# Expert weights eight rows to a partition, with the gathered tokens turned at a step of eight columns

## The reference

```python
def expert_choice_moe(h, w_router, w_gate, w_up, w_down):
    cap = EC_FACTOR * n // N_EXPERTS
    aff = jax.nn.softmax(jnp.einsum('bnd,de->bne', h, w_router), axis=-1)
    g, idx = lax.top_k(jnp.swapaxes(aff, 1, 2), cap)
    xs = jax.vmap(lambda hb, ib: hb[ib])(h, idx)
    hid = jax.nn.silu(jnp.einsum('becd,edf->becf', xs, w_gate)) * jnp.einsum('becd,edf->becf', xs, w_up)
    y = jnp.einsum('becf,efd->becd', hid, w_down) * g[..., None]
    return jax.vmap(lambda yb, ib: jnp.zeros((n, d)).at[ib.reshape(-1)].add(yb.reshape(-1, d)))(y, idx)
```

## Time and profile before

| | |
|---|---|
| median of 3 runs | 6196.72 us (6195.44 to 6198.15) |
| the profiled execution | 6197.2 us |
| its span, first to last instruction | 6195.5 us, so 1.7 us lie around it |
| mean granted clock of TensorE | 0.893 of full speed |
| TensorE busy | 5059.5 us, 82% of the span |
| VectorE, ScalarE, GpSimd busy | 31%, 18%, 17% |
| bytes by DMA | 491.31 MB, of which 32 x 3 loads of 2 MB are expert weights |

### The profile page before, as it was taken

How to read it: one execution, slowest core, us unless ns; L and a number is a source line. 1 busy time by engine, 2 the same in 40 slices (tenths; PEclk the granted TensorE clock), 3 DMA queues, 4 the chain that set the end, 5 groups by cost and what they waited for, 6 DMA issues and landing times. The chain is left out here.

```text
span 6195.5 us, 88364 instructions
## 1 busy us (share of the span) xinstructions
PE 5059.5 (82%) x37782; PEld 3656.2 (59%) x37782; DVE 1949.5 (31%) x2498; ACT 1102.5 (18%) x1784; POOL 1054.0 (17%) x782
## 2 busy tenths in 40 slices
PE   7689885888978879999695698799996956984897
PEld 2578764788833557777362276637664422763675
DVE  0206455444442142233303543241112035425001
ACT  1314212222221020000301132210001112312111
POOL 0120113434410212323000201101112002010011
PEclk8899997899998989999796799799997977996998
DMA  6220101000044111111000000276661100002985
GB/s 198 61 75 2 42 23 50 3 4 4 4 143 159 54 35 47 44 47 44 15 27 25 16 1 21 82 275 213 217 220 50 34 25 16 1 27 106 302 293 167
DMA packets 351297, 491.31 MB, mean 79 GB/s; under 512 B 56825, under 2 KB 210682, under 8 KB 351010
## 3 DMA queue, kind: packets, MB, share of 16 engines
q1 hardware_dynamic: 323650, 386.22, 18.8%
q0 software_dynamic: 25056, 92.40, 5.5%
q10 hardware_dynamic: 2304, 8.39, 0.3%
HBM read 427.71 MB, written 59.24 MB: 79 GB/s over the span
## 5 line engine op out<-in xcount | busy, mean ns | idle before, releaser
L2810 PE MATMUL l_experts_pY<-l_experts_wd,l_experts_hid 128*128 128x512 f32 (+1 forms) x768 | 356.2, 615 | 6.9 <-DVE l_experts_hid L2852 5.8
L1835 PE MATMUL l_in_ps<-l_mixT,l_in_w 128*128 128x512 f32 (+1 forms) x672 | 258.9, 549 | 62.7 <-DMA l_in_w<-in_w_in_dram 62.7
L2795 PEld LDWEIGHTS l_experts_pG<-l_experts_xT,l_experts_wg 128*128 128x128 f32 x2048 | 260.4, 194 | 21.9 <-issue 19.7
L2795 PE MATMUL l_experts_pG<-l_experts_xT,l_experts_wg 128*128 128x160 f32 (+1 forms) x2048 | 264.5, 291 | 1.6 <-ACT l_experts_xT L2840 1.6
L2795 PE MATMUL l_experts_pU<-l_experts_xT,l_experts_wu 128*128 128x160 f32 (+1 forms) x2048 | 258.7, 287 | 0.0
L2795 PEld LDWEIGHTS l_experts_pU<-l_experts_xT,l_experts_wu 128*128 128x128 f32 x2048 | 255.6, 191 | 0.0
L1835 PEld LDWEIGHTS l_in_ps<-l_mixT,l_in_w 128*128 128x128 f32 x672 | 129.3, 193 | 192.3 <-issue 124.8
L2810 PEld LDWEIGHTS l_experts_pY<-l_experts_wd,l_experts_hid 128*128 128x128 f32 (+1 forms) x768 | 125.8, 170 | 191.0 <-issue 186.7
L128 PE MATMUL mlp_ps<-h_hi,mlp_w_hi 128*128 128x512 f32 x512 | 200.5, 392 | 41.1 <-POOL mlp_w_lo L119 41.1
L128 PE MATMUL mlp_ps<-mlp_hid_hi,mlp_w_hi 128*128 128x512 f32 x512 | 203.8, 398 | 25.4 <-DVE mlp_hid_lo L1774 25.4
L128 PE MATMUL mlp_ps<-mlp_hid_lo,mlp_w_hi 128*128 128x512 f32 x512 | 202.7, 396 | 0.0
(11 more groups left out here) (527 smaller groups left out, 10552.2 us busy)
## 6 DMA issues: line engine op xcount, KB each, us to landing
l_experts_wg<-in_w_gate_dram SPq DMA_DIRECT2D x32, 2048.0 KB
l_experts_wu<-in_w_up_dram SPq DMA_DIRECT2D x32, 2048.0 KB, 14.2
l_experts_wd<-in_w_down_dram SPq DMA_DIRECT2D x32, 2048.0 KB, 11.1
b_mod_w_ada<-in_w_ada_dram SPq DMA_DIRECT2D x12, 2048.0 KB, 8.0
rec_out_w_ada<-in_w_ada_dram POOLq DMA_DIRECT2D x12, 2048.0 KB, 8.8
l_choose_w_ada<-in_w_ada_dram POOLq DMA_DIRECT2D x12, 2048.0 KB, 12.0
mlp_w<-in_w_mlp_up_dram SPq DMA_DIRECT2D x32, 512.0 KB, 4.0
mlp_w<-in_w_mlp_down_dram SPq DMA_DIRECT2D x32, 512.0 KB, 3.7
```

The source lines that it names most:

```text
L1835: mm = nc.tensor.matmul(ps[:, m % 2, c, 0:n], w[:, m % 2, k], hT[:, k, t0:t0 + n], start=(k == 0), stop=(k == KT - 1))
L2795: mm = nc.tensor.matmul(ps[:, f // 2, f % 2 * S:f % 2 * S + S], w[:, b, k, f * P:(f + 1) * P], xT[:, b, k], start=(k == 0), stop=(k == KT ...
L2810: mm = nc.tensor.matmul(pY[0:caps[n], c], hid[:, b, f, offs[n]:offs[n] + caps[n]], wd[:, b, f, c * 512:(c + 1) * 512], start=(f == 0), sto ...
```

## The change

The gate and up weights are laid so that row p * 8 + k goes to partition p, place k: the eight rows of a partition follow each other in DRAM, 16 KB in one piece. Since place k of partition p now holds another row of the weights, the turned tokens have to be laid the same way: transpose k takes the columns k, k + 8, k + 16, ... of the gathered rows (D = 1024, KT = 8) in place of 128 columns side by side. The down weights, the gathers, the scatters, the number of instructions on every engine and the waits are as before.

```diff
-                        sp.dma_start(wg[:, b], w_gate[bass.ds(e, 1)].rearrange("a (k p) f -> p (a k) f", p=P)
+                        sp.dma_start(wg[:, b], w_gate[bass.ds(e, 1)].rearrange("a (p k) f -> p (a k) f", k=KT)
                                      ).then_inc(g_full[b], 16)
-                        sp.dma_start(wu[:, b], w_up[bass.ds(e, 1)].rearrange("a (k p) f -> p (a k) f", p=P)
+                        sp.dma_start(wu[:, b], w_up[bass.ds(e, 1)].rearrange("a (p k) f -> p (a k) f", k=KT)
                                      ).then_inc(u_full[b], 16)
...
-                            tr = nc.tensor.transpose(pX[:, j // 2, o:o + cap], xs[n][:, b, k * P:(k + 1) * P],
+                            tr = nc.tensor.transpose(pX[:, j // 2, o:o + cap], xs[n][:, b, k:D:KT],
                                                      ident[0:cap, 0:cap])
```

## The result

The changed kernel takes 6235.27 us, the median of 4 runs (6230.03 to 6250.8), beside 6197.18 us (6195.44 to 6198.15, 4 runs) for the kernel before: a ratio of 1.0066, with an interval of 1.0048 to 1.0084. It is 38 to 41 us slower. That is inside the range of the prediction, but 24 us above its 6211, and most of what is lost stands in another place than the one forecast: the hit on the range is luck.

What follows compares the result with a forecast made beforehand. TensorE bounds layer 0 and the scatter-to-gather chain layer 1; 13.6 + 1.7 (loads) - 3.5 (transfers) + 2 (first gathers) = +13.8 us on 6197.2 gives 6211 us, range 6182 to 6262.

Steps and rivals of the forecast that it cites:

- rival 3: Turn's loads: the step costs more than a doubling, +80 ns a load or more, 6222 to 6264 us; chance 0.20.
- What bounds the kernel: Layer 0 is filled by TensorE work (452.75 of 455.2 us); layer 1 waits for gathers, 39.3 us in 14 times.
- Loads of the turn: Line 2785: strided loads double, +53 ns each, costing 13.6 us in layer 0 and 1.7 us in layer 1.
- that cover is used up: Layer 0, first half turn: VectorE's product hides at most 0.1 us an expert of the longer loads.
- 0.65 was the sign: Layer 1: four transposes of a half turn would take near 0.65 us if the forecast was right.
- Gate and up transfers, -3.5 us: Lines 2730 and 2732: 16 KB packets flow 4% faster, so layer 1's scatters land sooner; -3.5 us, ends 0 and -7.
- where I allow them no loss: Layer 1: gathers, whose packets stand among longer ones, lose nothing; landing late there would show the forecast wrong.
- First gathers, +2 us: Start of each stage, beside gate and up: +1 us a stage, +2 us, ends 0 and +9.
- (1): Turn's loads: the step costs nothing, 6196 us, 6190 to 6206; chance 0.28.
- (4): Gate and up transfers: a descriptor may stay one 2 KB row, leaving only the load's cost, 6212 us; chance 0.07.
- Rival 2: Layer 1: free step and shorter gather waits keep the clock from falling behind nine waits, 6178 us; chance 0.15.
- dividing line of 2.6 us: Layer 1: gather waits below about 2.6 us would keep the down products behind them at full clock.

Runs made afterwards that it cites:

- the parts alone: Kernel before with only the changed columns (turn): 6207.2 us, ratio 1.0013; with only the changed transfers and old columns: 6232.14 us, ratio 1.0053.
- the transfers alone: Changed gate and up transfers with the old side-by-side columns, against the kernel before: 6232.14 us, ratio 1.0053.
- v7: Changed kernel with each gather issued ahead of the scatter of the expert two before: 6170.21 us, ratio 0.9956 to the kernel before.
- v8: Changed transfers with dense loads, each gather issued ahead of the scatter of the expert two before: 6169.41 us, ratio 0.995 to the kernel before.

## Why the prediction was right or wrong

- **The number**: 6235 us lies in the range of 6182 to 6262 by luck. The range reached so far up for loads dearer than a doubling (rival 3), and the loads came out cheaper than that; the transfers, which were to give 3.5 us back, took some 33.
- **What bounds the kernel**: right in its views. That the transfers can act only through gathers and scatters was the right frame; the price put on that was not.
- **Loads of the turn**: a doubling, +53 ns, was near for one load: +44 ns in layer 0 (186 against 142), +45 over both. The term for layer 0, 13.6 us, was mis-sized: 6 us. Two steps of it failed. A transpose grew by 0.33 / 8 = 0.041 us, not by 0.053. And "that cover is used up" was wrong for the first half turn: the down products' first load began 2.01 us after its start in place of 1.89 (and in every other expert of before, 1.99), so 0.1 of its 0.33 us or less came through, and 0.3 of the second's. Before, that load came 0.14 us behind the turn's end, in after 0.07 us ahead of it: 0.2 us of cover were left and more, where the prediction allowed 0.1. In layer 1, 1.7 us were forecast, one load for each half turn. It cost half of that, 0.8 us: 0.06 us behind each wait, and nothing in the other half turn, which stayed at 0.60 us where 0.65 was the sign.
- **Gate and up transfers, -3.5 us**: wrong in sign. The rate did rise: in 4211 to 4219, with gate and up alone, 222 packets, 3.38 MB at 98.7% are 569 ns for 15.2 KB, 37.4 ns a KB against 41.4 in the earlier trace rows, a tenth and not 4%. It bought nothing, for nobody waits for weights. Two steps failed. One is that scatters land sooner for it, after 9.3 us: they landed after 9.9 us in the median (9.6 before), and GpSimd's waits for them grew by 9.0 us. The other is that gathers lose nothing in layer 1 ("where I allow them no loss"): four late ones cost 20 us, and with the slow groups behind them this was most of the loss. The margin that kept them safe was read nowhere: it is the 1.3 to 2.5 us between the gather's issue and the gate load's, and under 0.8 us a gather meets the long packets.
- **First gathers, +2 us**: measured +4.7 and +3.6. The bound was right (+4.5 a stage if engines share by packets), the choice was not. The nearly even bytes of the earlier trace rows were read as sharing mostly by bytes. The window was too wide for that reading: in 4136 to 4138 of the same trace, where both queues were at work, it is the packets that are nearly even (125 and 139) and not the bytes (0.45 and 0.28 MB). Sharing by packets should have been a rival of its own, with its price in both layers.
- **Sum**: +13.8 us was forecast on the profiled execution, of which loads 15.3. There the loads made some 7 us, the first gathers 8.3, and gathers and scatters of layer 1 with the slow groups 35. By their ratios the parts alone are +8 us (turn) and +33 us (transfers).
- **Rivals.** The step is not free (1), not dearer than a doubling (3), and the transfers are one piece (4). Rival 2 named the clock, but the waits grew where it needed them shorter, and 13 groups of 14 were slow. Its dividing line of 2.6 us does not hold in after: of four waits below it, three (2.34, 2.44 and 2.48 us) have a slow group behind them.
- **The last paragraph** named the place: "or if the gathers, whose packets stand among longer ones, land late in layer 1 as well, where I allow them no loss". It was the main case, and belonged in the sum.

What stays open: why a gather comes to be issued so near to the gate load. After one late gather the cycle's phase shifts; that this brings the next collision was not tried. Open too is why the lower clock sets in behind some waits and not behind others of the same length (in before, two of 2.89 us: a slow group at 5821.01 and none at 6079.23). The runs of after spread over 21 us in four runs, those of before over 17 us in 26, so a changing number of late gathers can be a part of the spread at most; this too is only argued.

## What to carry to other kernels

Before making a bulk transfer's pieces longer, list the small transfers that share its engines and are waited for: each of their packets can then stand behind one long piece. Take their issue times from the timeline and see how far they are from the bulk's; a margin that one late transfer can use up is none. To see how two queues share an engine, count packets and bytes in a window in which both are at work throughout. If a small transfer is on the path, first take it off (issue it early, give it a buffer of its own): here that was worth 38.6 us, and left 10 of the 38 us that the longer pieces cost.

## What the runs showed of the hardware that was not expected

- DMA engines share by packets: 142 packets of a gather passed beside 141 of the weights, though these had four times the bytes; with 2 KB pieces, 125 beside 139. In before and after, a gather of layer 1 took 4.2 to 4.7 us from issue to use where the gate load came 0.9 us or more behind it, 7.5 where 2 and 4 KB packets of earlier loads were still flowing (the first of before), and 9.4 to 11.8 among 16 KB packets.
- The passage from on time to late is short: over after and the transfers alone, six gate loads issued up to 0.78 us after the gather made it late, and none of those from 0.92 us on did. Between them, in v7 and v8, gate loads at +0.79, +0.82 and +0.87 us let the gather land after 8.5, 7.4 and 5.6 us.
- TensorE's weight load of 128 columns of float32 takes 142 to 150 ns dense in these turns and 186 to 208 ns at a step of two, four or eight; eight is the cheapest of the three.
- Loads in pieces of 2 KB (gate, up) and 4 KB (down) stall SyncE at the start of layer 0, 4 to 8 us an issue from the third on; with 16 KB pieces for gate and up all six went in 3.3 us. The stall may have protected the first gather; that was not tried by itself.
